# Moved products of small height, moved value tiles and identity products in a two-layer backbone with expert mixtures

## The reference

```python
for l in range(DEPTH):                      # 2
    h_lat = modulate(rmsnorm(x_lat, norm_mix_g[l]), mod[0], mod[1])
    h_ctx = modulate(rmsnorm(x_ctx, norm_mix_g[l]), mod_c[0], mod_c[1])
    y_lat, y_ctx = even_mixer(...) if l % 2 == 0 else odd_mixer(...)
    x_lat = x_lat + mod[2] * y_lat
    x_lat = x_lat + mod[5] * ec_moe(modulate(rmsnorm(x_lat, ...), mod[3], mod[4]), ...)
    # layer 0 alone: the same for x_ctx, with its own ec_moe
return rmsnorm(x_lat, norm_final_g)

# even mixer, the decays of its linear attention (rank 16, two directions)
la_f = log_sigmoid(lr_f @ decay_up[0] + decay_b[0]) / GLA_TAU
# odd mixer: recurrent half (xb, gates, gb) and spatial-gating half (u, v)
r = sigmoid(blockdiag(xc, gate_a_w[d])); i = sigmoid(blockdiag(xc, gate_x_w[d]))
h = linear_scan(exp(-8 r softplus(-lam)), sqrt(1 - a * a) * (i * xc));  y_rec = (h_0 + h_1) * gelu(gb)
gelu(u) * (sg_w @ layernorm(gelu(v)) + sg_b)

def ec_moe(h, w_router, w_gate, w_up, w_down):   # 16 experts, each takes its top tokens
    cap = 2 * T // 16                            # 128 latent tokens, 32 context tokens
    g, idx = lax.top_k(swapaxes(softmax(h @ w_router), 1, 2), cap)
    hid = silu(xg @ w_gate) * (xg @ w_up)
    out = hid @ w_down * g                       # scattered back and added
```

## Time and profile before

| what | value |
|---|---|
| median of 3 runs | 2625.16 us (2624.62 to 2626.14) |
| profiled execution | 2622.86 us, its span 2620.9 us |
| TensorE busy | 2358.0 us (90%) |
| VectorE, ScalarE, GpSimd busy | 1789.2, 1418.2, 186.9 us |
| mean granted clock of TensorE | 0.946 |
| even layer up to its experts | 0 to about 760 us |
| experts of layer 0 | about 760 to 1560 us |
| odd layer up to its experts | about 1560 to 2006 us |
| experts of layer 1, final norm | about 2006 to 2621 us |

### The profile page before, as it was taken

How to read it: one execution, slowest core, us unless ns; L and a number is a source line. 1 busy time by engine, 2 the same in 40 slices (tenths; PEclk the granted TensorE clock), 3 DMA queues, 4 the chain that set the end, 5 groups by cost and what they waited for, 6 DMA issues and landing times.

```text
span 2620.9 us, 33923 instructions
## 1 busy us (share of the span) xinstructions
PE 2358.0 (90%) x13028; PEld 1791.6 (68%) x13028; DVE 1789.2 (68%) x1987; ACT 1418.2 (54%) x1439; POOL 186.9 (7%) x220
## 2 busy tenths in 40 slices
PE   5999999789929999999999968998992999999994
PEld 3797787568716666666666647776872788888883
DVE  6523122454587888888888757566658899999995
ACT  6400112574525666665666645466452777777774
POOL 0000000000000110110101010000000111111110
PEclk9899999889959999999999988999995999999997
DMA  6024445655316887787877861111345999999995
GB/s 243 25 82 138 155 151 111 249 179 188 134 52 229 295 296 295 281 302 277 296 288 295 288 201 41 34 40 61 133 148 183 344 387 392 388 387 388 388 377 196
DMA packets 194339, 585.52 MB, mean 223 GB/s; under 512 B 19656, under 2 KB 64448, under 8 KB 187712
## 3 DMA queue, kind: packets, MB, share of 16 engines
q1 hardware_dynamic: 178688, 529.61, 54.5%
q0 software_dynamic: 12336, 48.24, 6.7%
q10 hardware_dynamic: 3216, 6.29, 0.7%
HBM read 536.88 MB, written 47.21 MB: 223 GB/s over the span
## 4 chain that ended last, share of the span: by engine, by line
PE 84%; DVE 7%; ACT 3%; DMA 3%; issue 1%; SPq 0%; POOLq 0%; ACTq 0%; POOL 0%; DVEq 0%
PE ps L1568 14%; PE ps L1570 14%; PE ps L1569 13%; PE ps L1581 7%; PE ps L564 5%; PE ps L565 5%; PE ps L566 5%; PE ps L787 3%; PE ps L789 2%; PE ps L788 2%; PE ps L506 1%; PE ps L540 1%; PE ps L1589 1%; PE ps L601 1%; PE ps L602 1%
## 5 line engine op out<-in xcount | busy, mean ns | idle before, releaser
L1777 DVE TENSOR_TENSOR R_H_r<-R_M,R_W_r 128x2048 fp32r<-128x2048 f32 x336 | 762.2, 2290 | 150.8 <-ACT R_W_r L1682 148.2
L1682 ACT CAST R_W_r<-R_M 128x2048 fp32r<-128x2048 f32 x336 | 640.5, 1914 | 224.1 <-PE ps L1570 84.1
L1570 PE MATMUL ps<-R_W_r,R_C_r 128*128 128x512 f32 x1536 | 608.7, 396 | 0.0
L1568 PE MATMUL ps<-R_W_r,bc_r 128*128 128x512 f32 x1024 | 414.3, 405 | 14.1 <-DVE R_C_r L1795 9.5
L1569 PE MATMUL ps<-R_H_r,bc_r 128*128 128x512 f32 x1024 | 405.2, 396 | 0.0
L1570 PEld LDWEIGHTS ps<-R_W_r,R_C_r 128*128 128x128 f32 x1536 | 290.4, 189 | 66.6
L564 PE MATMUL ps<-R_H_r,R_W_r 128*128 128x512 f32 (+1 forms) x632 | 233.9, 370 | 19.2 <-DVE R_W_r L911 8.8
L1568 PEld LDWEIGHTS ps<-R_W_r,bc_r 128*128 128x128 f32 x1024 | 193.8, 189 | 72.0 <-issue 17.2
L565 PE MATMUL ps<-R_C_r,R_W_r 128*128 128x512 f32 (+1 forms) x632 | 229.8, 364 | 0.0
L566 PE MATMUL ps<-R_H_r,R_W_r 128*128 128x512 f32 (+1 forms) x632 | 229.5, 363 | 0.0
L1569 PEld LDWEIGHTS ps<-R_H_r,bc_r 128*128 128x128 f32 x1024 | 194.0, 189 | 43.0
(11 more groups left out here) (319 smaller groups left out, 3703.8 us busy)
## 6 DMA issues: line engine op xcount, KB each, us to landing
R_M<-in_moe_w_gate SPq DMA_DIRECT2D x114, 1024.0 KB, 7.0
R_M<-in_moe_w_down SPq DMA_DIRECT2D x112, 1024.0 KB, 7.1
R_M<-in_moe_w_up SPq DMA_DIRECT2D x110, 1024.0 KB, 7.1
bc<-in_ada_w SPq DMA_DIRECT2D x28, 1024.0 KB, 4.9
R_H<-in_moe_w_up SPq DMA_DIRECT2D x18, 1024.0 KB
R_H<-in_moe_w_down SPq DMA_DIRECT2D x16, 1024.0 KB
R_H<-in_moe_w_gate SPq DMA_DIRECT2D x14, 1024.0 KB
R_W<-in_ev_w_in SPq DMA_DIRECT2D x25, 512.0 KB, 4.0
```

Source lines behind the costliest of these rows:

```text
L1568: pe.matmul(o, hi[:, k, :], wh[:, kk, cs], start=(k == 0), stop=False)
L1570: ins = pe.matmul(o, lo[:, k, 0:P], wh[:, kk, cs], start=False, stop=(k == KC - 1))
L1682: nc.scalar.copy(whi[j], raw[slot + j]).then_inc(unit_high_done, 1)
L1777: nc.vector.tensor_tensor(wlo[j], raw[slot + j], whi[j], ALU.subtract).then_inc(unit_low_done, 1)
```

## The change

The four decay projections move from ahead of the value tiles to behind tiles 1, 3, 5 and 7, and VectorE's program takes ten tile copies between the decays' work. In the odd layer's fills two value tiles stand ahead of the projection, and gb3 is split behind gb2. In layer 0's experts context matrices stand in pairs: gate and up ahead of an odd step's up units (and in step 0), up and the last expert's down behind an even step's up units, and behind an odd step's hidden transposes that step's down matrix and the next expert's gate. With `ahead=True` each unit of a context matrix waits for its own load. `context_unit_done` counts units instead of matrices, and SP's waits follow it or `expert_unit_used`. The hidden context columns get two buffers, the banks 6 and 7 change roles by parity (`context_banks`), and VectorE's `context_result` stands behind the hidden columns in odd steps. `keep_busy` is a run of products of the identity with itself, whose results nobody reads; it stands in six places, with 5 to 20 products.

```diff
+        xctx = [x[:, :, P:P + CAPC] for x in xT]
+        hctx = [R_C[:, 9728 + KC * CAPC * i:9728 + KC * CAPC * (i + 1)].rearrange("p (k c) -> p k c", k=KC) for i in range(2)]
...
-        fill = [[("gb", 0)] + [("v", i) for i in (0, 1, 2)], [("gb", 1)] + [("v", i) for i in (3, 4, 5)],
-                [("gb", 2)] + [("v", i) for i in (6, 7)], [("gb", 3)] + [("v", i) for i in (8, 9, 10)],
-                [("u", 0)] + [("v", i) for i in (11, 12, 13)], [("u", 1)] + [("v", i) for i in (14, 15)],
+        fill = [[("v", 0), ("v", 1), ("gb", 0), ("v", 2)], [("v", 3), ("v", 4), ("gb", 1), ("v", 5)],
+                [("v", 6), ("v", 7), ("gb", 2)], [("v", 8), ("v", 9), ("gb", 3), ("v", 10)],
+                [("v", 11), ("v", 12), ("u", 0), ("v", 13)], [("v", 14), ("v", 15), ("u", 1)],
                 [("u", 2)], [("u", 3)] + [("mix", t) for t in range(TL - 2)]]
...
         split_behind = {("xb", 1): ["xb3", "w0"], ("xb", 2): ["w1"], ("xb", 3): ["gb0"], ("v", 2): ["gb1"], ("v", 5): ["gb2"],
-                        ("v", 7): ["gb3"], ("ga", 3): ["w2", "w3"], ("v", 10): ["u0"], ("v", 13): ["u1"], ("ga", 6): ["u2", "u3"]}
+                        ("gb", 2): ["gb3"], ("ga", 3): ["w2", "w3"], ("v", 10): ["u0"], ("v", 13): ["u1"], ("ga", 6): ["u2", "u3"]}
...
+        def keep_busy(pe, bank, n):
+
+            for i in range(n):
+                pe.matmul(ps[:, bank, 0:P], ident[:, :], ident[:, :], start=True, stop=True)
...
             ada_rows(pe, 0)
+            keep_busy(pe, 6, 14)
...
             pe.wait_ge(lowrank_weights_loaded, 32)
-            for pd in range(4):
-                banks_free(pe, j)
-                for c0, cn in SPLIT:
-                    ins = pe.matmul(wide(j % 2, T)[:, c0:c0 + cn], decup[96:128, pd * P:(pd + 1) * P],
-                                    lrT[96:128, c0:c0 + cn], start=True, stop=True)
-                ins.then_inc(job_done, 1)
-                j += 1
...
                 v_tile(pe, x, t, 2 * half)
+                if x in (1, 3, 5, 7):
+                    pd = x // 2
+                    banks_free(pe, j)
+                    for c0, cn in SPLIT:
+                        ins = pe.matmul(wide(j % 2, T)[:, c0:c0 + cn], decup[96:128, pd * P:(pd + 1) * P],
+                                        lrT[96:128, c0:c0 + cn], start=True, stop=True)
+                    ins.then_inc(job_done, 1)
+                    j += 1
...
             pe.transpose(ps[:, 3, 0:ne], tkf[0:ne, :], ident[0:ne, 0:ne]).then_inc(ranked_transposed, 1)
+            keep_busy(pe, 0, 20)
...
+        def context_banks(e, odd):
+
+            return (7, 6, 7, 7, 6) if odd or isinstance(e, int) and e == 0 else (6, 7, 6, 6, 7)
...
-                        if l == 0:
-                            if j == 0:
-                                sp.wait_ge(context_matrix_done, matrix_number(m, e) - 1)
+                        if l == 1:
+                            sp.wait_ge(unit_low_done, u + j - 7)
+                        elif odd == (m != 0):
+                            sp.wait_ge(expert_unit_used, u + j - 7)
                         else:
-                            sp.wait_ge(unit_low_done, u + j - 7)
+                            sp.wait_ge(context_unit_done, 4 * matrix_number(m, e) - 8 + j + 1)
...
-            def context_matrix(m, e, odd, full, cbank):
+            def context_matrix(m, e, e2, odd, full, cbank, ahead=False):
 
                 slot = first_unit(l, m, e, odd)[1]
                 for j in range(4):
+                    if ahead:
+                        pe.wait_ge(*slot_loads(l, m, e, e2, odd, j))
                     w = raw[slot + j].rearrange("p (k n) -> p k n", k=2)
                     for kk in range(2):
                         for c in range(2):
                             q = 2 * kk + c
-                            ins = pe.matmul(ps[32 * q:32 * q + C, cbank, :], full[:, 2 * j + kk, P:P + C],
+                            ins = pe.matmul(ps[32 * q:32 * q + C, cbank, :], full[:, 2 * j + kk, :],
                                             w[:, kk, c * BANK:(c + 1) * BANK], start=(j == 0), stop=(j == 3))
-                ins.then_inc(context_matrix_done, 1)
-
-            def token_columns(n):
+                    ins.then_inc(context_unit_done, 1)
...
-                if C:
-                    down_read()
-                    context_matrix(0, e, odd, x, 6)
+                                if C:
+                                    pe.wait_ge(context_down_half_copied, n - 1)
+                                    pe.wait_ge(context_down_summed, n - 1)
+                        token_columns(n + 1, token_bank)
+                if not first:
+                    pe.wait_ge(hidden_low_done, n)
+                if C and (odd or first):
+                    context_matrix(0, e, e2, odd, xctx[odd], gate_bank)
                 if not last:
                     pe.wait_ge(tokens_by_vector, n + 2)
-                if not first:
-                    pe.wait_ge(hidden_low_done, n)
-                    if not second:
-                        pe.wait_ge(expert_rows_done, n - 1)
+                if not first and not second:
+                    pe.wait_ge(expert_rows_done, n - 1)
+                    if C and last:
+                        pe.wait_ge(context_down_half_copied, n - 1)
+                        pe.wait_ge(context_down_summed, n - 1)
+                if C and (odd or first):
+                    context_matrix(1, e, e2, odd, xctx[odd], up_bank, ahead=True)
                 for j in range(4):
                     unit(1, e, e2, odd, j, xl, xh, 2)
-                if C:
-                    context_matrix(1, e, odd, x, 7)
+                if C and not (odd or first):
+                    context_matrix(1, e, e2, odd, xctx[odd], up_bank)
+                    pe.wait_ge(context_gate_summed, n + 1)
+                    context_matrix(2, *before, hctx[1 - odd], down_bank, ahead=True)
...
+                if first:
+                    keep_busy(pe, 0, 9 if C else 5)
+                if last and not C:
+                    keep_busy(pe, 0, 10)
+                if C and odd:
+                    pe.wait_ge(context_gate_summed, n + 1)
+                    context_matrix(2, *before, hctx[1 - odd], down_bank)
+                    if not last:
+                        pe.wait_ge(hidden_low_done, n + 1)
+                        context_matrix(*matrix_order(e2 + 1, 0, l)[0], xctx[0], context_banks(e + 1, 0)[1], ahead=True)
+
+            token_columns(n0, 7)
+            keep_busy(pe, 0, 18)
             moe_steps(pe, step)
+            pe.wait_ge(expert_rows_done, n0 + NE - 1)
+            down(NE - 1, NE // 2 - 1, 1)
             if C:
                 pe.wait_ge(context_down_half_copied, n0 + NE - 1)
                 pe.wait_ge(context_down_summed, n0 + NE - 1)
-            pe.wait_ge(expert_rows_done, n0 + NE - 1)
-            down(NE - 1, NE // 2 - 1, 1, lambda: None)
+                context_matrix(2, NE - 1, NE // 2 - 1, 1, hctx[1], 6)
...
-                if C and not first:
-                    context_down(e - 1)
+                if C and not first and not odd:
+                    context_down(e - 1, down_bank)
                 act.wait_ge(hidden_transposed, n + 1)
                 nc.scalar.copy(hidh, ps[:, 2:4, :].rearrange("p b (k t) -> p (b k) t", k=4)).then_inc(hidden_high_done, 1)
+                if C and odd:
+                    context_down(e - 1, down_bank)
...
+                    if C and not odd:
+                        context_result(e - 1, down_bank)
...
                 ins.then_inc(hidden_low_done, 1)
+                if C and odd:
+                    context_result(e - 1, down_bank)
...
+            dve_v_copied(dve, 0)
+            dve_v_copied(dve, 1)
             dve_decay_in(dve, 0)
+            dve_v_copied(dve, 2)
+            dve_v_copied(dve, 3)
             dve_decay_in(dve, 1)
+            dve_v_copied(dve, 4)
             dve_decay_out(dve, own, 0)
+            dve_v_copied(dve, 5)
             dve_decay_in(dve, 2)
-            dve_v_copied(dve, 0)
+            dve_v_copied(dve, 6)
             dve_decay_out(dve, own, 1)
-            dve_v_copied(dve, 1)
+            dve_v_copied(dve, 7)
             dve_decay_in(dve, 3)
-            dve_v_copied(dve, 2)
+            dve_v_copied(dve, 8)
             dve_decay_out(dve, own, 2)
-            dve_v_copied(dve, 3)
-            dve_v_copied(dve, 4)
+            dve_v_copied(dve, 9)
             dve_decay_out(dve, own, 3)
             dve.wait_ge(lambda_log_done, 1)
             own.do(nc.vector.tensor_tensor(lruc[:, 0:8], lruc[:, 0:8], lruc[:, 8:16], ALU.add))
             nc.vector.tensor_scalar(lruc[:, 16:24], lruc[:, 0:8], -LRU_C, None, ALU.mult)
             nc.vector.tensor_scalar(lruc[:, 0:8], lruc[:, 0:8], LRU_C, None, ALU.mult).then_inc(lru_constants_done, 1)
```

93 lines of the change are left out of this document (47 added, 46 removed).

## The result

The changed kernel takes 2596.82 us (median of 4 runs, 2593.67 to 2599.1) beside 2625.65 us for the kernel before (4 runs): ratio 0.989, 95% interval 0.9873 to 0.9907, so 24 to 33 us faster. The forecast was 2603.8, range 2589 to 2617. The sign and the range held; the gain of 28.8 us was a third above the 21.4 forecast. The profiled execution of the changed kernel took 2593.67 us (span 2591.8), 3 us under its median; the one of before 2622.86. The two traces are 29.1 us apart in span.

The account below looks back on a forecast made before the run. TensorE's own work, idle gaps and stretches at 1.2 GHz were taken to set the end. Terms 8.5 + 2.8 + 5.7 + 5.6 - 1.2 = 21.4 us, off the median of 2625.16, gave 2603.8 us, range 2589 to 2617.

Parts of the forecast that it names:

- Part 1: Layer 0's decay projections among the value tiles: 8.5 us won, range 2 to 9.5.
- Part 2: Layer 0's context matrices in pairs: 2.8 us won over the experts, 5.7 more at the last one.
- Part 3: Identity products keep the clock up at the start and both layers' first experts: 5.6 us won, range 0 to 8.
- No low clock to mend: zero: Identity products in the last step of layer 1: nothing won, 0 us.
- Part 4: Odd layer, two value tiles ahead of the projection: 12.9 won, 14.1 lost, so 1.2 us lost.
- The stall at v8: Odd layer, w2 and w3 load behind gb3: TensorE idles 6.8 us, then loses 1.7 at half clock; 8.5 lost.
- The order at item 6: Odd layer, last two tiles ahead of u1: gx6 waits 4.2 us, 4 lost, and about 1.6 of clock.
- A: Clock stays as it is at the decay projections and identity products; these give 3 + 1, total 2614; chance 0.15.
- B: Identity products don't count as work, so the starts stay at 1.2 GHz: 2609.4 us; chance 0.07.
- C: Odd layer's stall at v8 does not come or is shorter; layer gains up to 10: 2594 us; chance 0.15.
- D: Layer 0's token columns come late, 3.2 us in each even step, price 19: 2623 us, no change; chance 0.1.
- E: Slower: each "ahead" context matrix waits before its four units; at 0.43 us each 2644 us; chance 0.05.

Follow-up runs that it names:

- e11: Changed kernel with the decay projections in twos, behind the second and sixth value tiles: 2601.56 us, ratio 0.9915 to the kernel before.
- e1: Kernel before with only the decay projections moved between layer 0's value tiles, VectorE's order with them: 2618.23 us beside 2623.67, ratio 0.9976.
- e9: Changed kernel with the weights w2 and w3 loaded and split ahead of gb3's: 2583.88 us, ratio 0.9844 to the kernel before.
- e10: e9's kernel with the root of the last two tiles' statistics behind u1's gelu on ScalarE: 2581.73 us, ratio 0.9834 to the kernel before.
- e4: Kernel before with only the odd layer's new order, two value tiles ahead of the projection: 2621.84 us, ratio 0.9988.
- e8: Changed kernel with the odd layer's order of before: 2596.95 us, ratio 0.9907 to the kernel before.
- e3: Kernel before with only the identity products (keep_busy and its five calls): 2614.18 us, ratio 0.9956.
- e7: Changed kernel with as many transposes of the identity in place of the identity products: 2594.9 us, ratio 0.9893 to the kernel before.
- e2: Kernel before with only layer 0's context matrices in pairs and the down one moved, no identity products: 2612.23 us, ratio 0.9956.

## Why the prediction was right, and where it was short

**Part 1, forecast 8.5, measured 8.65.** The counting of VectorE's passes against TensorE's tiles was right to the tile: one gap, at the thirteenth, 1.38 us for the 2.2 reckoned. The clock held. e11 shows that this was nearer to failing than the reasoning knew: the low end of my range for this part (2 us) was what two projections in a row come close to (2.8).

**Part 2, forecast 2.8 and 5.7, measured 3.2 and 6.4.** Two experts gain 0.43 us in the loop, 2.9 from the third expert to the fifteenth's end, and 0.3 more in the first two. The steps behind it were a saving of 0.8 less 0.45 of wait in the even step, and the wait is in the trace at 0.33 to 0.49. The profile names ScalarE's cast as its releaser, but the cast that this unit needs had long been done: VectorE ended its token columns at 864.29, and the unit began at 864.60. The last expert, from its gates to the end of its last context matrix, took 61.2 us for 67.6, with a wait of 0.57 us for the 0.6 forecast; the other 1.1 us of that row of the table lie in the transposes of the normed tiles behind it.

**Part 3, forecast 5.6, measured 9.4.** This is the term that was mis-sized, and most of what was missing. The step that failed is "the counts leave new idle time of 1 to 3 us behind several of them". At layer 1 none was left: the first 20 products began at half clock and took 6.5 us, 0.32 each, and the next 18 ran right into the first unit. At the start 0.66 us was left and at layer 0 1.39 us ahead of the first units, and the clock did not fall for either. The full price of every cold start came back, 1.7 us at the start, 0.9 and 4.0 at layer 0, and 2.8 at layer 1. My ceiling of 8 was low as well: I had counted the slow token transposes for layer 0 (1.97 us for eight) and left out the same 0.9 us at layer 1.

One reading of the forecast is wrong, and one zero of this part was luck. "TensorE has no gap over 0.3 us behind its first 15 us" is wrong for layer 1's experts: the trace of before has three gaps of 1.1 to 1.3 us up to 2061.4, and the one of 2.41 us ahead of the last down units. "No low clock to mend: zero" was true of that profile alone. In three of the five profiles without fillers there are 1.5 us to mend there (e1). So the trace of before was a lucky one in this place too, and these ten products won nothing between the two traces but would win 1.5 us in an execution like e1's.

**Part 4, forecast 1.2 lost, measured 0.1 won between the traces.** That the forecast came so near is luck in part, since two of its prices were wrong in opposite directions. The single waits came out as written: 1.01 us at v2 for "about 1", 7.09 at v8 for 6.8, 1.87 of clock there for 1.7, 4.35 at gx6 for 4.2, u2 11.4 us behind u1 for 11.2. But what they cost is another matter, and e9 and e10 measured it. The stall at v8 costs 11.0 us, not 8.5, with the low clock behind u3's wait in it, which only one profile shows without the stall. The order at item 6 costs 2.3, not 5.6. There the forecast priced a wait of TensorE in a stretch that TensorE doesn't bound. The chain of waits of the changed kernel shows it (start us, us, what; the piece named is the one that the next waited for; "issue" at 1780.33 is u1's gelu, which ScalarE's timeline has from 1780.30 to 1781.32):

```profile
1777.18 1.21 DVE vst L2217 x2
1779.01 1.28 ACT L2168
1780.33 1.01 issue
1781.34 1.28 ACT L2177
1782.64 1.33 ACT R_W L2177
...
1798.65 2.36 DVE R_M L2280
1801.16 0.65 issue
1802.37 1.34 ACT R_W L2177
```

VectorE's statistics, ScalarE's table and gelu of u1 (L2168), table and sigmoids of item 6, casts, VectorE's item 6, the sigmoid of item 7, and then u3. TensorE isn't in it, so its 4.35 us at gx6 hide behind work that would be waited for anyway, and only the table and the gelu (1.28 + 1.01 us) can be saved. The same view of the kernel before shows the chain on the same two engines from item 6 on, 1812.81 to 1830.8, so it could have been read:

```profile
1812.81 1.33 ACT R_W L2129
...
1818.24 1.50 DVE R_W L2218
...
1825.72 2.36 DVE R_M L2232
...
1829.44 1.34 ACT R_W L2129
```

Gains of 12.9 less 11.0 and 2.3 give 0.4 lost, beside 0.1 won in the traces. Timed against before the order wins 1 to 5 us (e4), and the likely reason was not in the forecast: the waits that it fills are those behind which the clock sometimes falls (e8).

**The sum.** The gap between 21.4 and 29.1 us is 3.8 for the identity products, 1.3 for the odd layer, 1.2 for parts 1 and 2, and 1.3 in stretches that no edit touches. Those last I can't put down to the change: the rest of the even layer alone varies between 396.5 and 400.2 us.

**The rivals.** A fell with e1 and e3. B is on plain products and fell with e3; that transposes hold the clock up as well is shown by e7. C (2594) came nearest in time, but by another way; its mechanism, an earlier load of w2 and w3, is e9. D and E didn't come: no gap of 3.2 us stands in the even steps (e2), and no idle time of TensorE stands ahead of any group of context products in the trace of the changed kernel.

## What to carry to other kernels

Where TensorE has a wait of known length ahead of a long stream, fill it with idle products up to within a us or so of its end: each cold start here gave back 1.4 to 3 us, and it is the filled time, not the number of instructions, that has to be sized. Reckon with fillers at half clock too: in one profile (e9) they ran slower than planned, passed the end of the wait and cost 1.6 us. Shallow products are better laid one by one between deep ones than side by side. Before a wait is priced, look in the chain of waits whether its engine is in the chain at that place; and look at a queue's order when a consumer is moved forward, since the load behind it must move too.

## What the runs showed of the hardware that was not expected

- Products 32 rows deep let the granted clock fall while TensorE is busy without a gap: 4.5 us of them in a row did (e11), 2.4 us between value tiles did in none of nine profiles, and 4.2 us of like products 128 rows deep left it at 1.0 (the gates of the odd layer).
- Transposes raise the clock as products do (e7: from 0.5 to 1.0 in a stretch of transposes alone).
- After a wait of 2.4 to 3.7 us the clock fell in some profiles and not in others, for the same instructions (u0 at 0.50 in e3 and 1.00 before; the last down units of layer 1 at 0.54 in e1 and 1.00 before). At u0, u1 and u3 it makes a stretch of 246 us vary by 5 us. The same work in the new order varied by 0.2: its waits of 7.1 and 4.4 us had half clock behind them in every profile.
